# Residual gate factors: 32-column selector sums and a broadcasting load in place of full-width selector matmuls

## The reference, cut to what matters

```python
mod = silu(c) @ w_mod[l] + b_mod[l]            # 6 blocks of 1024: sh1, sc1, g1, sh2, sc2, g2
x = x + g1 * rms_norm(y, g_post_mix)           # after the mixer
...
x = x + g2 * rms_norm(swiglu(h), g_post_ffn)   # after the feed-forward
```

## Time and profile before

| | |
|---|---|
| median of 3 runs | 1307.64 us (1306.75 to 1308.81) |
| span of the profiled execution, first to last instruction | 1305.8 us |
| PE busy in it | 1278.5 us, 98% |
| DVE busy | 813.1 us, 62% |
| ACT busy | 661.1 us, 51% |
| DMA, mean of 16 engines on the main queue | 46.6%, 150 GB/s |

### The profile page before, as it was taken

One profiled execution on the slowest core, in us unless ns is written; L12 is line 12 of the kernel. 1 busy time (PEld: TensorE's weight loads), 2 busy tenths in 40 slices (PEclk: granted clock), 3 DMA queues, 4 the chain that ended last, 5 costly groups with the idle time before them and its releaser, 6 DMA issues.

```text
span 1305.8 us, 20057 instructions
## 1 busy us (share of the span) xinstructions
PE 1278.5 (98%) x7715; PEld 1176.8 (90%) x7715; DVE 813.1 (62%) x1413; ACT 661.1 (51%) x1170; POOL 18.2 (1%) x38
## 2 busy tenths in 40 slices
PE   6999999999999999999999999999999999999998
PEld 4999999978889999998789999998897999999886
DVE  2697584764769877643368785747566885444424
ACT  5479873754454332342266888547444543333322
POOL 0000000200000000000000000001000000000000
PEclk9999999999999999999999999999999999999999
DMA  9645646323426766534325545463324464444531
GB/s 335 200 129 159 208 131 199 112 99 113 145 87 208 221 199 210 161 128 159 103 64 161 156 144 181 143 214 114 112 65 147 132 213 129 129 130 129 172 103 64
DMA packets 135058, 196.21 MB, mean 150 GB/s; under 512 B 9730, under 2 KB 68268, under 8 KB 134964
## 3 DMA queue, kind: packets, MB, share of 16 engines
q1 hardware_dynamic: 134964, 194.94, 46.6%
HBM read 193.03 MB, written 1.88 MB: 149 GB/s over the span
## 4 chain that ended last, share of the span: by engine, by line
PE 89%; DVE 4%; ACT 3%; DMA 1%; issue 1%; SPq 0%; DVEq 0%; ACTq 0%
PE bank L671 18%; PE bank L678 18%; PE bank L679 18%; PE bank L766 6%; PE bank L764 6%; PE bank L765 6%; PE bank L710 2%; DVE weight_low L1564 1%; PE bank L631 1%; PE bank L1058 1%; PE bank L1082 1%; ACT weight_high L1184 1%; PE bank L746 1%; PE bank L1067 1%; PE bank L902 1%
## 5 line engine op out<-in xcount | busy, mean ns | idle before, releaser
L678 PE MATMUL bank<-act_low,weight_high 128*128 128x384 f32 x1440 | 486.8, 338 | 0.7 <-DVE weight_low L1564 0.6
L679 PE MATMUL bank<-act_high,weight_low 128*128 128x384 f32 x1440 | 482.5, 335 | 0.0
L1564 DVE TENSOR_TENSOR weight_low<-raw,weight_high 128x1024 fp32r<-128x1024 f32 (+5 forms) x282 | 319.1, 1152 | 171.3 <-ACT weight_high L1184 171.0
L1184 ACT ACTIVATE weight_high<-raw 128x1024 fp32r<-128x1024 f32 (+5 forms) x282 | 273.3, 996 | 236.6 <-PE bank L766 74.1
L671 PE MATMUL bank<-act_high,weight_high 128*128 128x384 f32 x1440 | 315.1, 339 | 1.8 <-DVE t L1668 1.8
L678 PEld LDWEIGHTS bank<-act_low,weight_high 128*128 128x128 f32 x1440 | 270.9, 188 | 6.7 <-issue 4.9
L679 PEld LDWEIGHTS bank<-act_high,weight_low 128*128 128x128 f32 x1440 | 271.0, 188 | 0.0
L671 PEld LDWEIGHTS bank<-act_high,weight_high 128*128 128x128 f32 x1440 | 252.1, 188 | 8.4 <-issue 5.3
L764 PE MATMUL bank<-weight_high,hid_high 128*128 128x512 f32 x264 | 104.4, 395 | 0.0
L766 PE MATMUL bank<-weight_high,hid_low 128*128 128x512 f32 x264 | 102.8, 389 | 0.0
L765 PE MATMUL bank<-weight_low,hid_high 128*128 128x512 f32 x264 | 102.8, 389 | 0.0
(11 more groups left out here) (241 smaller groups left out, 1557.7 us busy)
## 6 DMA issues: line engine op xcount, KB each, us to landing
raw<-in_w_ffn_in SPq DMA_DIRECT2D x176, 256.0 KB, 3.7
mod_weight<-in_w_mod SPq DMA_DIRECT2D x80, 512.0 KB, 4.7
raw<-in_w_in SPq DMA_DIRECT2D x72, 512.0 KB, 4.3
raw<-in_w_ffn_out SPq DMA_DIRECT2D x44, 512.0 KB, 3.7
first_mod<-in_w_mod SPq DMA_DIRECT2D x4, 2048.0 KB, 13.9
raw<-in_w_o_lru SPq DMA_DIRECT2D x16, 512.0 KB, 3.7
raw<-in_w_out SPq DMA_DIRECT2D x16, 512.0 KB, 3.7
raw<-in_w_o_mla SPq DMA_DIRECT2D x8, 512.0 KB, 5.0
```

Source lines behind the costliest of these rows:

```text
L678: nc.tensor.matmul(o, view[0][:, kk, cols], low[:, k, :], start=False, stop=False)
L679: ins = nc.tensor.matmul(o, view[1][:, kk, cols], high[:, k, :], start=False, stop=k == total - 1)
L1184: nc.scalar.activation(high, w, ACT.Copy).then_inc(*AC.step())
L1564: nc.vector.tensor_tensor(low, w, high.bitcast(F), ALU.subtract).then_inc(*VE.step())
```

## The change

1. `gain_spread` becomes `gain_sums`: the stationary matrix has 32 columns, and the 512 columns of a block are cut into four pieces of 128, each on its own column group of the array (output partitions 32b and up). For the mixer the stationary matrix is `rep[:, 0:32]` (a one where partition mod 32 equals the column) and one matmul gives both conditions: 2 blocks x 4 pieces = 8 matmuls. For the feed-forward it is a window of `one_row` with a column of ones at place g: 2 x 2 x 4 = 16 matmuls. They run once, after pair 0 of `wo` and after pair 2 of `fo`. The result is rows: condition g on partition 32b + g.
2. DVE adds the bias and multiplies by `g_post` on a 128 x 256 tile (two instructions, `gain_rows`), where `gain_result` had four of 128 x 512.
3. SP stores those rows to a DRAM tensor with 4 DMAs (`gain_rows`, ahead of load `fi0[0]`, and ahead of `fo[14]`), waits until they have landed, and loads each condition's row to all 128 partitions with 2 DMAs of 512 KB (`gain_spread`, ahead of `fi0[1]` and `fo[15]`). `residual` waits for these.
4. Bias and `g_post` come as 8 small DMAs (`gain_inputs`, ahead of `wo[2]` and `fo[6]`) in place of 4 rows of bias and a 512 KB broadcast.
5. The additions of the bias rows on DVE (line 1596) and the making of `sel` go; POOL has three more small memsets at the start, and PE, ACT and DVE wait for them.

```diff
+                def gain_inputs(which):
+                    sp.wait_ge(*(at(PE, "scores", 23) if which == "mix" else at(PE, "fi10", 3)))
...
+                    for dst, src in zip(ROWS[which], (bias, post)):
+                        for b in range(4):
+                            sp.dma_start(dst[32 * b:32 * b + 32, :, :],
...
+                def gain_rows(which):
+                    sp.wait_ge(*at(VE, "gain_rows", which))
...
+                    for b in range(4):
+                        sp.dma_start(dst[:, :, b, :], ROWS[which][2][32 * b:32 * b + 2, :, :]).then_inc(*gain_full.step(by=16))
...
+                def gain_spread(which):
+                    sp.wait_ge(*at(gain_full, "rows", which))
...
+                    for g in range(2):
+                        sp.dma_start(GAIN[which][:, g, :], gain_rows_out[s, g:g + 1, :].to_broadcast([P, D])
...
-                    if n == of_job("wo")[4]:
+                    for which, job, first in (("mix", "wo", 2), ("ffn", "fo", 6)):
+                        if n == of_job(job)[first]:
+                            gain_inputs(which)
+                    if n == of_job("fi0")[0]:
                         gain_rows("mix")
-                    if n == of_job("fo")[8]:
+                    if n == of_job("fi0")[1]:
+                        gain_spread("mix")
+                    if n == of_job("fo")[14]:
                         gain_rows("ffn")
-                    if n == of_job("fi1")[0]:
-                        bias_rows()
+                    if n == of_job("fo")[15]:
+                        gain_spread("ffn")
...
+                def gain_sums(which, job):
+                    o = bank(f"{job}_b", 2)
+                    if which == "mix":
+                        pe.wait_ge(*at(VE, "partial", 5))
+                        pe.wait_ge(*at(VE, "mix", 7))
+                        for i, r in enumerate(GAINS[which]):
+                            for b in range(4):
+                                ins = nc.tensor.matmul(o[32 * b:32 * b + 32, P * i:P * i + P], rep[:, 0:32],
+                                                       partial[PARTIAL[r]][:, P * b:P * b + P], start=True, stop=True,
+                                                       skip_group_check=True)
...
+                        for i, r in enumerate(GAINS[which]):
+                            for g in range(2):
+                                for b in range(4):
+                                    ins = nc.tensor.matmul(o[32 * b:32 * b + 32, P * i:P * i + P], one_row[:, 31 - g:63 - g],
+                                                           total(r, g)[:, P * b:P * b + P], start=g == 0, stop=g == 1,
...
+                token_job("wo", hh, hl, "mix_low", {0: "mix"}, lambda: pe.wait_ge(*at(VE, "mix", 5)))
+                token_job("fo", hidh, hidl, "hid_low", {2: "ffn"}, lambda: banks_free("fo_b"))
...
+                    nc.vector.tensor_tensor(row[:, :, :], sums, bias[:, :, :], ALU.add).then_inc(*VE.step())
+                    own()
+                    nc.vector.tensor_tensor(row[:, :, :], row[:, :, :], post[:, :, :], ALU.mult).then_inc(*VE.step("gain_rows", which))
...
                     own()
+                    ve.wait_ge(*at(gain_full, "spread", post))
                     for a in TILES:
...
                 lows("wo", 4)
-                gain_result(4, "wo")
-                lows("wo", 6)
-                gain_result(5, "wo")
+                gain_rows("mix", "wo")
...
+                lows("fo", 10)
+                gain_rows("ffn", "fo")
                 lows("fo", 15)
```

More of the change, by code:

```diff
@@ L247, in program @@
         ss = sb("sums", [P, 24])
-        pick = sb("pick", [P, 2])
+        one_row = sb("one_row", [P, 63])
         qkv_flat = qkv[:, :, :].rearrange("p c t -> p (c t)")
@@ L486, in gain_rows @@
                     sp.sem_inc(sync_passed, 1)
[L487 to L493, removed]
-                    sp.sem_inc(sync_passed, 1)
-                    for r in GAINS["ffn"]:
-                        sp.dma_start(partial[r - 10][0:1, :], A["b_mod"][l:l + 1, 512 * r:512 * r + 512]
+                    r0 = GAINS[which][0]
@@ new lines, in gain_inputs @@
+                    bias = A["b_mod"][l:l + 1, 512 * r0:512 * r0 + D]
+                    post = A["g_post_mix" if which == "mix" else "g_post_ffn"][l:l + 1, :]
+                    for dst, src in zip(ROWS[which], (bias, post)):
+                        for b in range(4):
+                            sp.dma_start(dst[32 * b:32 * b + 32, :, :],
+                                         src.rearrange("a (h n) -> a h n", h=2)[:, :, P * b:P * b + P].to_broadcast([32, 2, P])
+                                         ).then_inc(*gain_full.step(by=16))
@@ L497, in bias_rows @@
+                def gain_spread(which):
+                    sp.wait_ge(*at(gain_full, "rows", which))
+                    sp.sem_inc(sync_passed, 1)
+                    s = 2 * l + (which == "ffn")
+                    for g in range(2):
+                        sp.dma_start(GAIN[which][:, g, :], gain_rows_out[s, g:g + 1, :].to_broadcast([P, D])
                                      ).then_inc(*gain_full.step(by=16))
-                    gain_full.also("bias")
+                    gain_full.also("spread", which)
@@ L731, in mod_fold @@
                     ins.then_inc(*PE.step("fold", r))
[L733 to L741, removed]
-                    else:
[L743 to L747, removed]
+                def gain_sums(which, job):
[8 more added lines that the diff above has]
+                                                       skip_group_check=True)
+                    else:
+                        pe.wait_ge(*at(VE, "summed", 11))
+                        for i, r in enumerate(GAINS[which]):
[3 more added lines that the diff above has]
+                                                           total(r, g)[:, P * b:P * b + P], start=g == 0, stop=g == 1,
+                                                           skip_group_check=True)
+                    ins.then_inc(*PE.step("gain_sums", which))
                 def token_job(job, high, low, ready, after, begin_b):
@@ L1589, in sum_quarter @@
                     VE.also("used", n)
[L1590 to L1598, removed]
+                    if i == 3:
+                        VE.also("summed", r)
                 jobs_reads = dict(jobs)
@@ L1641, in mod_result, with gain_rows @@
                     nc.vector.tensor_tensor(mod[:, 4 * r:4 * r + 4, :], o, bias, ALU.add).then_inc(*VE.step("mod", r))
[L1643 to L1654, removed]
+                def gain_rows(which, job):
+                    bias, post, row = ROWS[which]
+                    ve.wait_ge(*at(gain_full, "inputs", which))
+                    ve.wait_ge(*at(PE, "gain_sums", which))
+                    sums = bank(f"{job}_b", 2)[:, 0:2 * P].rearrange("p (h n) -> p h n", h=2)
+                    nc.vector.tensor_tensor(row[:, :, :], sums, bias[:, :, :], ALU.add).then_inc(*VE.step())
+                    own()
+                    nc.vector.tensor_tensor(row[:, :, :], row[:, :, :], post[:, :, :], ALU.mult).then_inc(*VE.step("gain_rows", which))
                 def vec2(name):
@@ L1966, in _ @@
                     nc.vector.tensor_copy(par[:, :], bank("outs", 3)[:, 0:NA + NB]).then_inc(*VE.step("par_next"))
[L1967 to L1970, removed]
                 else:
```

37 lines of the change are left out of this document (17 added, 20 removed).

## The result

The changed kernel takes 1298.2 us (median of 4 runs, 1296.89 to 1298.91) against 1307.56 us before (4 runs, 1306.75 to 1308.81): ratio 0.9926, 95% interval 0.9914 to 0.9937. Measured again beside a later version, it took 1298.17 against 1307.73 us, ratio 0.9927 (0.9914 to 0.9939). That is 9.4 us less where 10.0 were forecast. The span of the profiled execution fell from 1305.8 to 1295.1 us.

A forecast was written before the change was run, and what follows sets the result against it. PE was taken to bound the kernel: -14.1 us removed, +3.9 for the new sums, +0.2 for a late spread make -10.0, from 1307.64 to 1297.6 us. The range was 1296.0 to 1301.0.

The forecast's parts named there:

- What bounds the kernel: Whole kernel: PE, busy 98% of the span, sets the end; a microsecond off PE in `wo` or `fo` comes off the end.
- What is removed, 14.1 us: In `wo` and `fo`, eight chain entries of two full-width float32 matmuls go, 1.76 us each, 14.1 us in all.
- What PE gets, 3.9 us: New summing matmuls in `wo` and `fo`, priced after line 710: 0.71 and 1.22 us a batch, 3.9 us in all.
- Rival B: Column groups of the sums don't overlap: 0.27 us a matmul, 13.0 us in all, so 1306.5 us, no change; chance 0.04.
- DVE: In `wo`, four instructions of 0.69 us become two of 0.42; DVE waits for nothing, and `fo` gains nothing either.
- SP, inputs: Eight issues of about 0.31 us, 2.5 us, ahead of `wo[2]` and `fo[6]`; hidden, so no cost.
- SP, rows and spread in `wo`: Spread through DRAM behind `wo` lands at 358.8 to 363.2, middle 361.0, deadline 361.7; costs 0.2 us likeliest, 3.0 at most.
- The sign of being wrong: Behind `wo`: DVE idle over 2 us for a DMA at the first `y`, or batches over 2 us, would mean wrong.
- The price of a broadcast: In `wo`, one 512 KB broadcast needs 1.5 to 3.7 us of the queue, two 3 to 7.4.
- A: Spread in `wo` lands moderately late, 362.7 to 364: 1 to 2.3 us a layer, 1299.4 to 1302.0 us; chance 0.12.
- C: Round trip through DRAM in `wo` is slow, one us per us and layer past 361.7; 1314 at landing 370; chance 0.04.
- likeliest case: Whole kernel: the main forecast, own range 1296.5 to 1299.2 us, the upper end a delay of 0.8 a layer; chance 0.80.

The follow-up runs named there:

- e4: The changed kernel with the four full-width float32 matmuls added back behind the sums of each job, into an unread bank: 1311.31 us, ratio 1.0027.
- e2: The changed kernel with all pieces of the sums sent to one column group (output partitions 0 to 31) instead of four: 1305.36 us, ratio 0.998.
- e8: The changed kernel as it is, measured again on one chip beside a later version: 1298.17 us, ratio 0.9927.
- e3: The changed kernel with two more 512 KB broadcasts to an unused tile ahead of the spread, mixer half only: 1304.37 us, ratio 0.9975.
- e7: The changed kernel with 2 stores of the rows instead of 4 and the sample condition broadcast first on its own semaphore: 1296.24 us, ratio 0.9917.
- e5: The changed kernel with the rows stored to DRAM by 2 DMAs, one for each condition, instead of 4: 1297.52 us, ratio 0.9927.
- e6: The changed kernel with the sample condition's broadcast sent first, on its own semaphore: 1296.54 us, ratio 0.9919.

## Why the prediction was right, step by step

- **What bounds the kernel.** Right. PE stayed at 98% of the span, and the four stretches that PE's instructions shortened are 9.5 us of the span.
- **What is removed, 14.1 us.** Right, if a little high: e4 put it back and it cost 13.6 to 13.7 with the hidden 0.6 counted, 0.85 or 0.86 a matmul where 0.88 was used.
- **What PE gets, 3.9 us.** Right: 0.57 + 0.2 and 1.01 + 0.2 are 1.98 us a layer, 1.93 forecast. By the stretches the sums cost a little less: in `wo` 3.40 removed less 2.77 gained is 0.63, in `fo` 3.41 less 2.27 is 1.14, together 1.77 a layer and 3.5 us in all. So both terms of the sum were 0.4 to 0.5 too high and cancel: 13.6 - 3.5 = 10.1 where 10.2 was forecast. That the net is right to a tenth is in part luck. The row of line 710 was the right one to price it by. The upper bound without overlap, 13.0 us, was too high: e2 measured 0.23 us a matmul, not 0.27, which makes 24 x 0.23 x 2 = 11.0. The record of 1.90 us for 7 runs past the start of the next matmul, which stands 1.65 us behind, 0.24 each. Rival B was excluded by e2: without overlap the batches would have been 1.86 and 3.61 us.
- **DVE.** Right: two instructions of 0.42 and 0.43 us, straight behind a low part, as forecast.
- **SP, inputs.** The mechanism was right, the size wrong. The issues were put at 0.31 us each, after rows of one partition. With several rows of 512 bytes in one DMA they take 0.45 to 0.68, so eight take 4.8 us in `fo` of layer 0 instead of 2.5 (576.93 to 581.71) and 3.7 in layer 1. It still costs nothing: `fo` between the seams gained its 2.3 us to a tenth.
- **SP, rows and spread in `wo`.** The step that was mis-sized. The deadline was right to 0.1 us: 14.5 us behind the sums by the forecast, 14.65 by the table above. The stores' issues took 2.7 us instead of 1.4. Their landing took 1.6 us from the start of the last issue, where 2.0 from its end was put in, so the broadcasts went out only 0.4 us late (354.1 on the time axis of the trace before, 353.7 forecast). They landed at 362.3 on that axis (361.2 on their own), 1.3 us behind the middle of the forecast and within its 358.8 to 363.2; so most of the lateness is in the transfer. For the 0.8 us of receipt in that sum no run has a row of its own. Slack of 0.7 us hid half of it, and 0.56 was left in one layer, where 0.2 in all was put in: 0.4 of the 0.5 us by which the traces fall short of 10.0. Between the forecast of 1297.6 and the median of 1298.2 it can't be told from noise, since e8 has 0.1 us of lateness and the same median. That lateness past the deadline costs one for one, which was only argued from the earlier trace rows, is shown by the six seams, by the three edits that remove it and by e3 (2.5 and 3.3 us of delay, 3.2 and 3.8 of cost, where the clock comes on top).
- **The sign of being wrong.** One of them fired: DVE's idle time put down to the DMA was 3.37 us in layer 0 and 2.69 in layer 1, and over 2 us was to mean that the prediction is wrong. The time was right all the same, so the sign was badly set. DVE idles 1.16 us there without any wait for the DMA (e7), and up to the deadline it can idle 2.0 more at no cost (14.65 - 12.65). The sign should have been the landing against the deadline.
- **The price of a broadcast.** Wrong in its reason. The slow stretch in the earlier trace rows was put down to the broadcast of `g_post_mix`, 1.5 to 3.7 us each; e3 measured 1.3 to 1.6. So a broadcast isn't slow by itself; that the landing comes late because of the loads that share the engines fits e5's rates and isn't shown alone. What makes that stretch slow in the kernel before is open.
- **Rivals A and C.** A didn't happen: 0.56 us in one layer lies in the likeliest case's own range, up to 0.8 a layer. For C, e3 shows the mechanism at work; in its trace the price of one for one was too low, since the clock fell as well once PE had waited 3 us.
- **Start.** POOL's memsets cost nothing: PE waits for the same DMA at the start, 3.6 us against 3.5.

## What to carry to other kernels

In these runs a float32 matmul that sums over partitions costs by its moving columns, not by its output columns (512 columns: 0.86 us for 128 outputs, 4 x 0.23 for 32). So if few outputs are wanted, cut the moving columns into pieces and give each its own column group, in turn, so that four run at once; replicate the result by DMA, which PE doesn't pay for. Before moving such a step to a round trip through DRAM, write down the deadline of its first user, not its start in the trace before (the removed work makes that earlier), count the issues of the small DMAs on the path, and look at which load is issued just ahead of the broadcasts. When the landing is close to the deadline, fewer stores or the needed row first took it off here.

## What the runs showed of the hardware that was not expected

- **The granted clock fell after a short idle time.** In e3 PE waited 3.06 us in the seam of layer 0, and the clock was 0.50 from 374.5 to 381.4; the same was seen in layer 1 behind 3.27 us (1012.8 to 1019.6). In the seams of the changed kernel, with idle pieces of 0.55, 0.59 and 1.17 us, it stays at 1.00. So in this trace a late transfer cost 0.5 to 0.7 us a layer more than its lateness.
- **The start isn't the same twice, and the clock is in it.** The timeline of PE, kernel before and, below it, changed:

```profile
14.31 3.64 PE L844 MATMUL bank<-first_mod,cs 128*32 128x512 f32 x16 [0.69 <-DMA first_mod<-in_w_mod]
17.88 2.05 PE L631 MATMUL bank<-rstd,x 128*128 128x128 f32 x8
```

```profile
14.21 2.56 PE L868 MATMUL bank<-first_mod,cs 128*32 128x512 f32 x16 [0.65 <-DMA first_mod<-in_w_mod]
16.70 1.16 PE L650 MATMUL bank<-rstd,x 128*128 128x128 f32 x8
```

The same batch takes 1.92 us when it comes again (at 21.75, changed). The windows say 1.00 for the clock here, but the trace's first entry on the clock stands at 19.8 us before and at 15.5 in the changed kernel, so ahead of it the 1.00 isn't a reading. The lengths, 2.05 against 1.16 for one group, are those of the lower level, as in e3 (1.92 against 1.06). By that the kernel before left the lower level later, and at the second batch it was 2.1 us behind (23.82 against 21.75). Then the clock went to 0.50 once more, from 30.0 to 33.4 before and from 25.8 to 32.6 in the changed kernel, which brings the difference down to 1.3 (35.42 against 34.14) and to 1.1 at the sums. In e7 it didn't fall there at all, and e7 has its sums first, at 344.98. None of this is the change's: e6, which has it, starts like the kernel before (3.64 us for the first batch, sums at 347.20 against 347.17). Such a difference stands in every later time, so spans of two profiled executions can't be compared to a microsecond; stretches between marks can.
- **Issuing a small DMA costs by its shape.** 0.31 us for one row, 0.45 to 0.68 us for the pieces of 512 bytes here. Two stores of four partitions took 1.18 us, 0.59 each, where the four of two partitions took 0.67 each.
